# Moving the first layer's filter products and spectra into the start-up of a two-layer flow step

## The chip, the core and the metric

The kernel runs on one core of one Trainium2 chip. The metric is the time on the device in microseconds (us), here the median of three runs. TensorE (PE) multiplies matrices, VectorE (DVE), ScalarE (ACT) and GpSimd (POOL) work element by element, and SyncE (SP) issues the loads.

## The reference

Two trunk layers, each a mixer and a mixture of experts, over 128 context tokens and 256 latent tokens, 1024 features, float32. What the change touches is the filter of the Hyena group inside the mixer. It depends on the layer's parameters and on fixed tables alone, not on the tokens:

```python
def hyena_filter_spectrum(L, p):
    ...
    feats = jnp.concatenate([t[:, None], jnp.cos(ang), -jnp.sin(ang)], axis=-1)
    fr = p['hy_freq'].astype(f32)
    hid = jnp.sin(fr * (feats @ p['hy_w1'].astype(f32) + p['hy_b1'].astype(f32)))
    hid = jnp.sin(fr * (hid @ p['hy_w2'].astype(f32) + p['hy_b2'].astype(f32)))
    filt = (hid @ p['hy_w3'].astype(f32)).reshape(L, 2, HYENA_ORDER, D_HYENA)
    ...
    filt = filt * window[:, None, None, :]
    fwd, bwd = filt[:, 0], filt[:, 1]
    k = jnp.concatenate([fwd, jnp.zeros((1, HYENA_ORDER, D_HYENA), f32), bwd[:0:-1]], axis=0)
    return jnp.fft.rfft(k, axis=0)

def trunk_layer(x, cond, p, l, ctx_kv, ang):
    mod = cond @ p['w_mod'] + p['b_mod']
    sh1, sc1, g1, sh2, sc2, g2 = jnp.split(mod[:, None, :], N_MOD, axis=-1)
    h = rms_norm(x, p['g_pre_mix']) * (1.0 + sc1) + sh1
    y, k, v = mixer(h, p, l, ctx_kv, ang)
    ...
```

The spectrum is first used in `hyena_group`, after the projection `u = h @ p['w_in']`: the tokens' spectrum is multiplied by it, twice.

## The kernel before

The program is written out by hand: each engine has one list of instructions in a fixed order, and the engines wait for one another on counters (semaphores) by `wait_ge`. An engine that waits holds back everything behind it in its list. The loads of the start-up all go through SyncE's list, in the order written; `weight_in`, `mod_in` and the constants use one queue.

**Start-up of layer 0.** Twelve modulation chunks of 2 MB per layer (`mod_chunk`, L680) give the shifts, scales and gates; chunks 0 to 3 give the shift and scale of the mixer's norm. Their products gather in PSUM banks 6 and 7, are copied to SBUF (`mod_rows`), turned into columns by TensorE (`mod_columns`, L661), copied (`mod_column`) and applied while the transposed, normalised tokens (`to_features`, L824, banks 0 to 5) are copied out of PSUM by ScalarE and VectorE (`features`, L1320 and L1605). The small filter network is `hidden` (L691 and L694 on TensorE, L1867 to L1870 on VectorE, a sine on ScalarE).

**Projection stage.** 19 tiles (`u_tile`, `u_high` and `u_rest`, lines L896 to L924) in the loop over `i`, in the order `ORDER`, with PSUM banks 3 to 5. Tiles 2 to 9 are products of split weights: ScalarE copies the high part (`high`, L1449) into one of three buffers, and VectorE (tiles 2, 3) or GpSimd (tiles 4 to 9, L634) subtracts it. Between the tiles TensorE's list holds the filter work, for both layers alike: behind tiles 3, 4, 5 the filter blocks (`filters`, L703: two products of 128x512 into banks 1 and 2), which VectorE multiplies by the windows and adds and subtracts (L1879 to L1882, tiles FA and FB, which lie in QKV); behind tiles 6, 7, 8 the spectra (`spectra`, L717 and L721, banks 1 and 2), which ScalarE copies to KS (in KSYS, L1431). Behind tiles 9, 10 and 12 follow the turn, the spectrum and the inverse of the tokens (`z_turn`, `z_spectra`, `z_conv`), and again behind 13, 14 and 16. Each filter block waits for VectorE to have emptied the banks, each spectrum for ScalarE.

After that come attention, the output projection and the experts; layer 1 has the same stages, with `hidden` behind its first tiles.

Of the kernel before, what the change touches and what calls it, by code (L numbers as in the profile page):

```python
# [28 lines left out]
P = 128  # L29
# [34 lines left out]
_n = 0  # L64
for _name, _w in (("ident", 128), ("cond", 16), ("mean", 128), ("cf2", 512), ("sf2", 512), ("cf1", 128), ("sf1", 128),
                  ("ci2", 512), ("si2", 512), ("ci1", 128), ("si1", 128), ("win", 768), ("win0", 768),
                  ("cos", 64), ("sin", 64), ("tri", 64), ("iota", 384), ("before", 128), ("tokid", 3)):
    CONST[_name] = (_n, _n + _w)
    _n += _w
NCONST = _n  # L70
FIRST = CONST["cond"][1]
PAR = {}
# [29 lines left out]
def build(nc, I, O):  # L102
    lam_init = [0.8 - 0.6 * math.exp(-0.3 * l) for l in range(DEPTH)]
    with ExitStack() as ctx:
# [146 lines left out]
        NH3 = len(HALVED)  # L251
        FTB = ((0, 2, 4), (6, 0, 2))
        ROWB = (6, 6, 4, 6)
        COLB = (6, 5, 4, 5)
# [31 lines left out]
        def sem(name):  # L286
# [4 lines left out]

        const_in, x_in, par_in, ctx_in, kv_out, y_out = map(
            sem, ("const_in", "x_in", "par_in", "ctx_in", "kv_out", "y_out"))
        chunk_in = [sem(f"chunk_in{i}") for i in range(SLOTS + 1)]
# [116 lines left out]
        def _(sp):  # L411
# [37 lines left out]
            for l in range(DEPTH):  # L449
                if l == 0:  # L450
                    mod_in(0)
                    sp.dma_start(PR[:, :], I["par"][0]).then_inc(par_in, 16)
                    mod_in(1)
                    sp.dma_start(X[:, :, :], I["x"]).then_inc(x_in, 16)
                    mod_in(2)
                    mod_in(3)
                weight_in(l, "f1")
                if l == 0:
                    sp.dma_start(CST[:, FIRST:], I["consts"][:, FIRST:]).then_inc(const_in, 16)
                    sp.wait_ge(mod_used, 3)  # L460
# [191 lines left out]
        def _(pe):  # L652
# [43 lines left out]
            def filters(l, t):  # L696

                if t == 0:
                    pe.wait_ge(a_hid, 2 * l + 2)
                else:  # L700
                    pe.wait_ge(d_filt, K_FILT * l + 4 * t)
                for half in range(2):
                    mm = nc.tensor.matmul(PS[1 + half][:, :], HID[:, 4, t * P:(t + 1) * P],  # L703
                                          par("w3", 64)[:, half * 512:(half + 1) * 512], start=True, stop=True)
                mm.then_inc(pe_filt, 1)

            def spectra(l, q):

                if q == 0:
                    pe.wait_ge(const_in, 32)  # L710
                    pe.wait_ge(d_filt, K_FILT * l + K_FILT)
                else:
                    pe.wait_ge(a_spec, 6 * l + 2 * q)
                for part, f in ((0, FA), (1, FB)):
                    if q == 0:
                        w = cst("cf1" if part == 0 else "sf1")
                        mm = nc.tensor.matmul(PS[1 + part][:, :], w, f[:, 0, :], start=True, stop=True)  # L717
                    else:
                        w = cst("cf2" if part == 0 else "sf2").rearrange("p (t f) -> p t f", t=2)
                        for t in range(2):  # L720
                            mm = nc.tensor.matmul(PS[1 + part][:, :], w[:, t, (q - 1) * P:q * P], f[:, 1 + t, :],  # L721
                                                  start=(t == 0), stop=(t == 1))
                mm.then_inc(pe_spec, 1)

            def z_turn(l, o):

                if o == 0:
                    pe.wait_ge(a_spec, 6 * l + 6)
# [88 lines left out]
            def to_features(l, r, t):  # L817

                pe.wait_ge(d_xn, 6 * l + 3 * r + t + 1)
                if r == 1 and t > 0:  # L820
                    features_done(l, 1, t - 1)
                for half in range(2):
                    for k in range(4):
                        mm = nc.tensor.transpose(PS[FTB[r][t] + half][:, k * P:(k + 1) * P], XNK[r][:, t, 4 * half + k, :], ident)  # L824
                    mm.then_inc(pe_hT, 1)
# [324 lines left out]
            for l in range(DEPTH):  # L1150

                if l == 0:
                    pe.wait_ge(const_in, 16)
                    mod_chunk(0)
                    mod_chunk(1)
                    hidden(l, 0)
                    mod_chunk(2)
                    hidden(l, 1)
                    pe.wait_ge(d_arg, 8)
                    for t in range(NT):  # L1160
                        to_features(l, 0, t)
                    mod_chunk(3)
                    mod_columns(0)
                else:
                    for t in range(NT):
# [3 lines left out]
                for i in range(19):  # L1169
# [120 lines left out]
        def _(act):  # L1290
# [136 lines left out]
            def spectra(l, q):  # L1427

                act.wait_ge(pe_spec, NT * l + q + 1)
                for part in range(2):  # L1430
                    own.sig(sc.activation(KS[:, q, part, :, :].rearrange("p o n -> p (o n)"), PS[1 + part][:, :], ACT.Copy), a_spec)  # L1431

# [44 lines left out]
            for l in range(DEPTH):  # L1477
                act.wait_ge(par_in, 16 * (l + 1))
                if l == 0:
                    for t in range(NT):  # L1480
                        squares(l, 0, t)
                    hidden(l, 0)
                    hidden(l, 1)
                    mod_rows(0)
                    mod_column(0)
                    act.wait_ge(d_mod, 3)
                    for t in range(NT):
                        features(l, 0, t)
                else:
                    for t in range(NT):  # L1490
# [19 lines left out]
                for i in range(19):  # L1510
# [3 lines left out]
                    if 1 <= i < 7:  # L1514
                        high(l, i + 1)
                    if 6 <= i < 9:
                        spectra(l, i - 6)
# [72 lines left out]
        def _(dve):  # L1590
# [281 lines left out]
            def filters(l, t):  # L1872
# [3 lines left out]
                two = lambda ap: ap.rearrange("p (o n) -> p o n", o=2)  # L1876
                dve.wait_ge(const_in, 32)
                dve.wait_ge(pe_filt, NT * l + t + 1)
                sig(v.tensor_tensor(two(FW), two(PS[1][:, :]), win[:, t, :].unsqueeze(1).to_broadcast([P, 2, 256]), ALU.mult), d_filt)  # L1879
                do(v.tensor_tensor(two(BW), two(PS[2][:, :]), win0[:, t, :].unsqueeze(1).to_broadcast([P, 2, 256]), ALU.mult), d_filt)  # L1880
                sig(v.tensor_tensor(FA[:, t, :], FW, BW, ALU.add), d_filt)
# [102 lines left out]
            for l in range(DEPTH):  # L1984
# [274 lines left out]
```

## Time and profile before

| What | Value |
|---|---|
| runs | 1751.35, 1750.44, 1751.37 us; median 1751.35 |
| profiled execution, span | 1745.4 us from its first to its last instruction |
| profiled execution, own time | not recorded apart; the median lies 5.95 us above the span |
| TensorE busy | 1661.9 us, 95% |
| VectorE, ScalarE, GpSimd busy | 642.6 (37%), 387.3 (22%), 222.8 us (13%) |
| mean granted TensorE clock | 0.982 |
| TensorE's chain share | 89% |

The profile is of one execution. A row of a timeline gives the start in us from the span's start, the duration, the engine and line, what is written from what is read, how many instructions the row merges, and in brackets the engine's idle time before it and what ended that. One float32 matmul of the program stands in it as two records; L12 is line 12 of the kernel. Where a row's records overlap, the duration of the chain of waits is the one that adds up.

### The profile page before, as it was taken

To read this page: it belongs to the slowest core of one execution; us is meant where nothing else is said; L and a number is where in the kernel's file an instruction comes from. 1 tells how busy PE (TensorE), PEld (TensorE's weight loads), DVE (VectorE), ACT (ScalarE), POOL (GpSimd) and SP (SyncE) were. 2 spreads that over 40 slices of the span, in tenths; PEclk is the share of its full clock that TensorE was granted. 3 is DMA by queue.
4 is the path that set the end of the run, shared out by engine and by line. 5 is a ranking of instruction groups with operands and counts; after the bars stand their busy time and mean duration, and the time that the engine had idled before them with its cause. 6 is when DMAs were issued, how large, how long until landed. Compare 5 with 4: busy or idle time off the path is not lost.

```text
span 1745.4 us, 22336 instructions
## 1 busy us (share of the span) xinstructions
PE 1661.9 (95%) x8468; PEld 821.2 (47%) x8468; DVE 642.6 (37%) x1697; ACT 387.3 (22%) x842; POOL 222.8 (13%) x217
## 2 busy tenths in 40 slices
PE   4999889989999999999979998998999999999997
PEld 2765344644444444444447553555434444444443
DVE  2479372522222222222256765442322222222222
ACT  2410343221111111111152104431111111111111
POOL 0200010011111111111113000101111111111110
PEclk7999999999999999999989999999999999999999
DMA  9312753399999999999932229017899999999994
GB/s 403 133 54 102 279 210 145 126 403 374 417 403 413 417 388 419 420 420 419 381 128 97 103 97 375 23 60 310 338 418 416 396 420 396 412 419 420 419 420 166
DMA packets 77291, 530.52 MB, mean 304 GB/s; under 512 B 10880, under 2 KB 14080, under 8 KB 21632
## 3 DMA queue, kind: packets, MB, share of 16 engines
q1 hardware_dynamic: 67392, 503.90, 70.7%
q0 software_dynamic: 9792, 25.18, 3.7%
q8 instruction: 69, 1.13, 0.3%
q14 instruction: 38, 0.31, 0.1%
HBM read 533.76 MB, written 5.77 MB: 309 GB/s over the span
## 4 chain that ended last, share of the span: by engine, by line
PE 89%; DVE 4%; DMA 4%; ACT 2%; issue 1%; SPq 0%; POOL 0%; DVEq 0%; ACTq 0%
PE PSB L932 30%; PE PSB L941 15%; PE PSB L924 7%; PE PSB L986 6%; PE PSB L987 5%; PE PSB L974 4%; PE PSB L860 4%; DMA RING<-in_wmod 2%; PE PSB L896 1%; PE PSB L959 1%; PE PSB L919 1%; PE PSB L680 1%; PE PSB L906 1%; PE PSB L897 1%; DMA RING<-in_exp_w_up 1%; PE PSB L948 1%
## 5 line engine op out<-in xcount | busy, mean ns | idle before, releaser
L932 PE MATMUL PSB<-WB,EX 128*32 128x512 f32 (+2 forms) x1408 | 431.9, 598 | 0.6 <-DMA RING<-in_exp_w_up 0.6
L932 PE MATMUL PSB<-RING,EX 128*32 128x512 f32 (+2 forms) x1344 | 417.2, 598 | 1.7 <-DVE EX L1790 1.7
L941 PE MATMUL PSB<-RING,AT 128*32 128x512 f32 (+2 forms) x720 | 227.9, 599 | 4.8 <-ACT GROW L1299 3.7
L1808 DVE TENSOR_TENSOR YL<-PSB,YH 128x512 fp32r<-128x512 f32 x136 | 94.1, 692 | 353.8 <-ACT YH L1380 353.8
L941 PE MATMUL PSB<-WB,AT 128*32 128x512 f32 (+2 forms) x704 | 210.8, 596 | 0.0
L564 POOL TENSOR_SCALAR SCAT<-CST,LSTT 128x384 fp32r<-128x384 f32 x68 | 85.1, 1251 | 833.0 <-PE PSB L987 832.8
L932 PEld LDWEIGHTS PSB<-WB,EX 128*32 128x32 f32 (+2 forms) x1408 | 113.1, 126 | 136.3 <-issue 136.3
L986 PE MATMUL PSB<-YH,SCAT 128*128 128x512 f32 x408 | 171.6, 421 | 2.8 <-DVE YL L1808 2.8
L1790 DVE COPY EX<-PSB 128x512 f32<-128x512 f32 x68 | 47.1, 692 | 317.4 <-PE PSB L974 317.4
L932 PEld LDWEIGHTS PSB<-RING,EX 128*32 128x32 f32 (+2 forms) x1344 | 105.8, 124 | 122.5 <-issue 122.5
L987 PE MATMUL PSB<-YL,SCAT 128*128 128x512 f32 x408 | 161.0, 395 | 0.0
L1380 ACT ACTIVATE YH<-PSB 128x512 fp32r<-128x512 f32 x136 | 81.2, 597 | 239.5 <-PE PSB L941 239.5
L924 PE MATMUL PSB<-RING,HT 128*128 128x512 f32 x288 | 125.9, 592 | 0.0
L974 PEld LDWEIGHTS PSB<-CST,XG 128*128 128x128 f32 x544 | 58.9, 141 | 107.4 <-issue 105.4
L941 PEld LDWEIGHTS PSB<-RING,AT 128*32 128x32 f32 (+2 forms) x720 | 62.7, 129 | 78.4 <-issue 74.5
L1373 ACT ACTIVATE SGM<-PSB 128x256 f32<-128x256 f32 x68 | 26.1, 384 | 312.7 <-PE PSB L932 312.7
L941 PEld LDWEIGHTS PSB<-WB,AT 128*32 128x32 f32 (+2 forms) x704 | 58.4, 126 | 72.5 <-issue 72.0
L974 PE MATMUL PSB<-CST,XG 128*128 128x128 f32 x544 | 88.7, 286 | 1.4 <-ACT EX L1355 1.4
L556 POOL DMA_INDIRECT XG<-h_rows,IDX x68 | 74.7, 1098 | 113.3 <-DVE LSTW L1760 89.5
L986 PEld LDWEIGHTS PSB<-YH,SCAT 128*128 128x128 f32 x408 | 77.6, 190 | 21.1 <-issue 4.9
L860 PE MATMUL PSB<-RING,YT 128*128 128x512 f32 x192 | 86.5, 598 | 0.0
L924 PEld LDWEIGHTS PSB<-RING,HT 128*128 128x128 f32 x288 | 54.3, 190 | 63.0 <-issue 62.2
(286 smaller groups left out, 1856.6 us busy)
## 6 DMA issues: line engine op xcount, KB each, us to landing
RING<-in_exp_w_gate SPq DMA_DIRECT2D x64, 1024.0 KB, 12.4
RING<-in_exp_w_up SPq DMA_DIRECT2D x64, 1024.0 KB, 14.7
RING<-in_exp_w_down SPq DMA_DIRECT2D x64, 1024.0 KB, 13.1
WB<-in_exp_w_gate SPq DMA_DIRECT2D x64, 1024.0 KB, 11.7
WB<-in_exp_w_up SPq DMA_DIRECT2D x64, 1024.0 KB, 14.4
WB<-in_exp_w_down SPq DMA_DIRECT2D x64, 1024.0 KB, 13.3
RING<-in_wmod SPq DMA_DIRECT2D x16, 2048.0 KB, 10.6
KSYS<-in_wmod SPq DMA_DIRECT2D x8, 2048.0 KB, 10.4
```

The lines of the kernel that those rows point to most:

```text
L556: pool.indirect_dma_start(XG[:, s % 2, :], None, h_rows, bass.IndirectOffsetOnAxis(ap=IDX[:, s:s + 1], axis=0), bounds_check=TOK - 1, oob_ ...
L564: nc.gpsimd.tensor_scalar(SCAT[:, s % 2, :], cst("iota"), LSTT[:, s:s + 1], None, ALU.is_equal).then_inc(p_scat, 1)
L860: mm = nc.tensor.matmul(PS[YB[0][t] + hf][:, :], YT[:, f, t * P:(t + 1) * P], w[:, f, :], start=(f == 0), stop=(f == 7))
L924: mm = nc.tensor.matmul(PS[3 + i % 3][:, :], HT[:, k, t * P:(t + 1) * P], w[:, k, :], start=(k == 0), stop=(k == KD - 1))
L932: mm = nc.tensor.matmul(PS[6][s0:s0 + w, :].rearrange("p (w f) -> p w f", w=2), e[:, k, s0:s0 + w], rawgu[n % NBUF][:, k], start=(k == 0), ...
L941: mm = nc.tensor.matmul(dst[s0:s0 + w, :], AT[:, j, s0:s0 + w], rawdn[n % NBUF][:, hf, j], start=(j == 0), stop=(j == 1))
L974: mm = nc.tensor.transpose(PS[7][:, c * P:(c + 1) * P], XG[:, s % 2, k * P:(k + 1) * P], ident)
L986: nc.tensor.matmul(PS[piece][:, :], w, YHb[s % 2][:, cols], start=False, stop=False, skip_group_check=True)
L987: mm = nc.tensor.matmul(PS[piece][:, :], w, YLb[s % 2][:, cols], start=False, stop=True, skip_group_check=True)
L1380: sc.activation(YHb[s % 2][:, hf * 512:(hf + 1) * 512], PS[6 + hf][:, :], ACT.Copy).then_inc(a_yh, 1)
L1790: v.tensor_copy(EX2[:, s % 2, 4:8, :].rearrange("p k s -> p (k s)"), PS[7][:, :]).then_inc(e_high, 1)
L1808: v.tensor_tensor(YLb[s % 2][:, hf * 512:(hf + 1) * 512], PS[6 + hf][:, :], YHb[s % 2][:, hf * 512:(hf + 1) * 512].bitcast(F32), ALU.subtr ...
```

## The change

For layer 0 alone, the three filter blocks and the three spectra leave the loop over `i` and stand in the start-up, among the modulation chunks; both `hidden` steps stand ahead of chunk 0, and chunk 3 ahead of the transposes. Each filter block and each spectrum of layer 0 gets PSUM banks of its own (`FILTB`, `SPECB`), so most waits between them fall away; the transposes of tokens 0 and 1 wait for the copies of spectra 0 and 1, whose banks they take over. The constants are laid out anew in three parts with semaphores of their own (`win_in`, `dft_in`, `const_in`); the parameters and the windows load ahead of chunk 0, the Fourier tables behind chunk 1, the rest behind the first projection weights. VectorE does both `hidden` steps and the window products before it normalises the tokens; ScalarE does the sines before the squares, copies spectra 0 and 1 before `mod_rows`, and spectrum 2 behind `features`. Layer 1 is as before.

```diff
-for _name, _w in (("ident", 128), ("cond", 16), ("mean", 128), ("cf2", 512), ("sf2", 512), ("cf1", 128), ("sf1", 128),
-                  ("ci2", 512), ("si2", 512), ("ci1", 128), ("si1", 128), ("win", 768), ("win0", 768),
+for _name, _w in (("ident", 128), ("cond", 16), ("win", 768), ("win0", 768), ("cf2", 512), ("sf2", 512), ("cf1", 128),
+                  ("sf1", 128), ("mean", 128), ("ci2", 512), ("si2", 512), ("ci1", 128), ("si1", 128),
...
+        FILTB = ((0, 2, 4), (1, 1, 1))
+        SPECB = ((0, 2, 6), (1, 1, 1))
...
                 if l == 0:
+                    sp.dma_start(PR[:, :], I["par"][0]).then_inc(par_in, 16)
+                    sp.dma_start(CST[:, FIRST:WINDOWS], I["consts"][:, FIRST:WINDOWS]).then_inc(win_in, 16)
                     mod_in(0)
-                    sp.dma_start(PR[:, :], I["par"][0]).then_inc(par_in, 16)
                     mod_in(1)
+                    sp.dma_start(CST[:, WINDOWS:FORWARD], I["consts"][:, WINDOWS:FORWARD]).then_inc(dft_in, 16)
                     sp.dma_start(X[:, :, :], I["x"]).then_inc(x_in, 16)
...
                 if l == 0:
-                    sp.dma_start(CST[:, FIRST:], I["consts"][:, FIRST:]).then_inc(const_in, 16)
+                    sp.dma_start(CST[:, FORWARD:], I["consts"][:, FORWARD:]).then_inc(const_in, 16)
                     sp.wait_ge(mod_used, 3)
...
                 if t == 0:
                     pe.wait_ge(a_hid, 2 * l + 2)
-                else:
+                elif l > 0:
                     pe.wait_ge(d_filt, K_FILT * l + 4 * t)
                 for half in range(2):
-                    mm = nc.tensor.matmul(PS[1 + half][:, :], HID[:, 4, t * P:(t + 1) * P],
+                    mm = nc.tensor.matmul(PS[FILTB[l][t] + half][:, :], HID[:, 4, t * P:(t + 1) * P],
...
                 if q == 0:
-                    pe.wait_ge(const_in, 32)
+                    pe.wait_ge(dft_in, 16)
                     pe.wait_ge(d_filt, K_FILT * l + K_FILT)
-                else:
+                elif l > 0:
                     pe.wait_ge(a_spec, 6 * l + 2 * q)
+                elif q == 2:
+                    pe.wait_ge(a_col, 1)
...
                 pe.wait_ge(d_xn, 6 * l + 3 * r + t + 1)
+                if l + r == 0 and t < 2:
+                    pe.wait_ge(a_spec, 2 * t + 2)
...
                 if l == 0:
                     pe.wait_ge(const_in, 16)
+                    hidden(l, 0)
+                    hidden(l, 1)
                     mod_chunk(0)
+                    filters(l, 0)
                     mod_chunk(1)
-                    hidden(l, 0)
+                    filters(l, 1)
+                    filters(l, 2)
+                    spectra(l, 0)
                     mod_chunk(2)
-                    hidden(l, 1)
-                    pe.wait_ge(d_arg, 8)
+                    spectra(l, 1)
+                    mod_chunk(3)
                     for t in range(NT):
                         to_features(l, 0, t)
-                    mod_chunk(3)
                     mod_columns(0)
+                    spectra(l, 2)
...
-                    if 3 <= i < 6:
+                    if l > 0 and 3 <= i < 6:
                         filters(l, i - 3)
-                    if 6 <= i < 9:
+                    if l > 0 and 6 <= i < 9:
                         spectra(l, i - 6)
...
                 if l == 0:
+                    hidden(l, 0)
+                    hidden(l, 1)
                     for t in range(NT):
                         squares(l, 0, t)
-                    hidden(l, 0)
-                    hidden(l, 1)
+                    spectra(l, 0)
+                    spectra(l, 1)
                     mod_rows(0)
                     mod_column(0)
                     act.wait_ge(d_mod, 3)
                     for t in range(NT):
                         features(l, 0, t)
+                    spectra(l, 2)
...
                     scalars()
                     hidden(l, 0)
+                    hidden(l, 1)
+                    for t in range(NT):
+                        filters(l, t)
                     for t in range(NT):
                         normalise(l, 0, t)
-                    hidden(l, 1)
...
                 low(l, 1)
                 if l > 0:
                     hidden(l, 1)
-                for t in range(NT):
-                    filters(l, t)
+                    for t in range(NT):
+                        filters(l, t)
+                dve.wait_ge(const_in, 32)
                 short(l, 0)
```

TensorE's list before, from the program's start to the first projection tile (L919); L680 are modulation chunks of eight products, L691 and L694 the two `hidden` products, L824 the transposes, L661 `mod_columns`:

```order
L680 MATMUL PSB<-RING,COND 32x512 x16
L691 MATMUL PSB<-PR 64x384
L680 MATMUL PSB<-RING,COND 32x512 x8
L694 MATMUL PSB<-CO,PR 64x384
L824 MATMUL PSB<-CST,YT 128x128 x24
L680 MATMUL PSB<-RING,COND 32x512 x8
L661 MATMUL PSB<-FOLD,GROW 128x4 x8
L919 MATMUL PSB<-HT,RING 128x384 x16
```

The same stretch of TensorE's list now; L684 are the chunks, L707 the filter blocks (two products each), L723 and L727 the spectra, L833 the transposes, L665 `mod_columns`, L928 the first tile:

```order
L695 MATMUL PSB<-PR 64x384
L698 MATMUL PSB<-CO,PR 64x384
L684 MATMUL PSB<-RING,COND 32x512 x8
L707 MATMUL PSB<-PR,CO 128x512 x2
L684 MATMUL PSB<-RING,COND 32x512 x8
L707 MATMUL PSB<-PR,CO 128x512 x4
L723 MATMUL PSB<-QKV,CST 128x512 x2
L684 MATMUL PSB<-RING,COND 32x512 x8
L727 MATMUL PSB<-QKV,CST 128x512 x4
L684 MATMUL PSB<-RING,COND 32x512 x8
L833 MATMUL PSB<-CST,YT 128x128 x24
L665 MATMUL PSB<-FOLD,GROW 128x4 x8
```

Behind these twelve rows stand spectrum 2 (L727, four products) and the first tile; filter blocks 1 and 2 stand together, and spectrum 0 ahead of chunk 2.

SyncE's list of loads before, from the start to the last first-stage weights; columns are float32, 128 rows each:

```order
L448 DMA CST<-in_consts 128x144
L417 DMA RING<-in_wmod 128x4096
L452 DMA PR<-in_par 128x2100
L417 DMA RING<-in_wmod 128x4096
L454 DMA X<-in_x 128x3072
L417 DMA RING<-in_wmod 128x4096 x2
L429 DMA RING<-in_wfm 128x4096
L459 DMA CST<-in_consts 128x4931
L429 DMA RING<-in_wfm 128x2048
L429 DMA RING<-in_wfm 128x4096
```

The same stretch of SyncE's list now:

```order
L450 DMA CST<-in_consts 128x144
L453 DMA PR<-in_par 128x2100
L454 DMA CST<-in_consts 128x1536
L419 DMA RING<-in_wmod 128x4096 x2
L457 DMA CST<-in_consts 128x1280
L458 DMA X<-in_x 128x3072
L419 DMA RING<-in_wmod 128x4096 x2
L431 DMA RING<-in_wfm 128x4096
L463 DMA CST<-in_consts 128x2115
L431 DMA RING<-in_wfm 128x2048
L431 DMA RING<-in_wfm 128x4096
```

The parameters (2100 columns) and the windows (1536) have moved ahead of all modulation chunks, the Fourier tables (1280) ahead of X; the loads are the same bytes in all.

## Rows read from the trace of the kernel before

**Rows 1.** TensorE timeline: start us, us, line, out<-in, count, idle before it
```profile
8.95 3.28 PE L680 MATMUL PSB<-RING,COND 128*32 128x512 f32 x16 [8.95 <-DMA RING<-in_wmod]
16.30 3.64 PE L680 MATMUL PSB<-RING,COND 128*32 128x512 f32 x16 [4.07 <-DMA RING<-in_wmod]
19.87 1.54 PE L691 MATMUL PSB<-PR 17*64 17x384 f32 x2
24.89 3.64 PE L680 MATMUL PSB<-RING,COND 128*32 128x512 f32 x16 [3.48 <-DMA RING<-in_wmod]
...
31.59 4.56 PE L824 MATMUL PSB<-CST,YT 128*128 128x128 f32 x24 [2.12 <-DVE CO L1870]
36.08 1.92 PE L680 MATMUL PSB<-RING,COND 128*32 128x512 f32 x16
38.72 1.95 PE L661 MATMUL PSB<-FOLD,GROW 128*128 128x4 f32 x16 [0.72 <-ACT GROW L1411]
46.01 1.65 PE L919 MATMUL PSB<-HT,RING 128*128 128x384 f32 x2 [5.34 <-ACT HT L1320]
```

**Rows 2.** DMA issues before 130 us: count, KB each, us to landing
```profile
RING<-in_wmod SPq DMA_DIRECT2D x4, 2048.0 KB, 11.9
...
CST<-in_consts SPq DMA_DIRECT2D x1, 2465.5 KB, 20.8
X<-in_x SPq DMA_DIRECT2D x1, 1536.0 KB, 17.4
PR<-in_par SPq DMA_DIRECT2D x1, 1050.0 KB, 9.7
```

**Rows 3.** Stretches: us, TensorE busy (records), granted clock, DMA share, GB/s
```profile
28.00:29.00 1.00, 1.00 (x6) 0.60 1.04 442
...
35.00:36.00 1.00, 1.00 (x8) 0.68 0.97 414
...
42.00:43.00 1.00, 0.00 (x0) 0.73 0.96 410
...
217.00:218.00 1.00, 0.49 (x4) 1.00 0.88 377
218.00:219.00 1.00, 0.08 (x1) 1.00 1.15 492
```

**Rows 4.** Chain of waits in two stages: start us, us, what
```profile
66.53 1.92 PE PSB L703 x4
...
85.44 1.72 PE PSB L717 x4
...
91.39 3.43 PE PSB L721 x8
...
106.59 0.65 PE PSB L734 x6
...
196.67 11.68 DMA RING<-in_wmod
```

**Rows 5.** TensorE's timeline once the first projection tiles are under way
```profile
49.65 8.55 PE L919 MATMUL PSB<-HT,RING 128*128 128x384 f32 x26
```

**Rows 6.** VectorE's timeline, window multiplications of the third filter block
```profile
81.21 0.69 DVE L1879 TENSOR_TENSOR QKV<-PSB,CST 128x512 f32<-128x512 f32 x1 [3.16 <-PE PSB L703]
81.82 0.68 DVE L1880 TENSOR_TENSOR QKV<-PSB,CST 128x512 f32<-128x512 f32 x1
82.53 1.18 DVE L1881 TENSOR_TENSOR QKV<-QKV 128x512 f32<-128x512 f32 x1
83.64 0.68 DVE L1882 TENSOR_TENSOR QKV<-QKV 128x512 f32<-128x512 f32 x1
```

**Rows 7.** GpSimd's timeline at the same place: a weight split
```profile
80.77 2.40 POOL L634 TENSOR_TENSOR RINGL<-RING,GROWH 128x1024 fp32r<-128x1024 f32 x1 [3.87 <-ACT GROWH L1449]
```

**Rows 8.** ScalarE's timeline: a weight split's copy, and a spectrum's two copies
```profile
79.63 1.06 ACT L1449 ACTIVATE GROWH<-RING 128x1024 fp32r<-128x1024 f32 x1
...
87.19 1.09 ACT L1431 ACTIVATE KSYS<-PSB 128x512 f32<-128x512 f32 x2 [0.60 <-PE PSB L717]
```

More of the change, by code:

```diff
@@ L70 @@
 NCONST = _n
-FIRST = CONST["cond"][1]
+FIRST, WINDOWS, FORWARD = CONST["cond"][1], CONST["win0"][1], CONST["sf1"][1]
 PAR = {}
@@ L289, in sem @@
             return sems[name]
-        const_in, x_in, par_in, ctx_in, kv_out, y_out = map(
-            sem, ("const_in", "x_in", "par_in", "ctx_in", "kv_out", "y_out"))
+        const_in, win_in, dft_in, x_in, par_in, ctx_in, kv_out, y_out = map(
+            sem, ("const_in", "win_in", "dft_in", "x_in", "par_in", "ctx_in", "kv_out", "y_out"))
         chunk_in = [sem(f"chunk_in{i}") for i in range(SLOTS + 1)]
@@ L716, in spectra @@
                         w = cst("cf1" if part == 0 else "sf1")
-                        mm = nc.tensor.matmul(PS[1 + part][:, :], w, f[:, 0, :], start=True, stop=True)
+                        mm = nc.tensor.matmul(PS[SPECB[l][q] + part][:, :], w, f[:, 0, :], start=True, stop=True)
                     else:
@@ L720, in spectra @@
                         for t in range(2):
-                            mm = nc.tensor.matmul(PS[1 + part][:, :], w[:, t, (q - 1) * P:q * P], f[:, 1 + t, :],
+                            mm = nc.tensor.matmul(PS[SPECB[l][q] + part][:, :], w[:, t, (q - 1) * P:q * P], f[:, 1 + t, :],
                                                   start=(t == 0), stop=(t == 1))
@@ L727, in z_turn @@
                 if o == 0:
+                    pe.wait_ge(const_in, 32)
                     pe.wait_ge(a_spec, 6 * l + 6)
@@ L1430, in spectra @@
                 for part in range(2):
-                    own.sig(sc.activation(KS[:, q, part, :, :].rearrange("p o n -> p (o n)"), PS[1 + part][:, :], ACT.Copy), a_spec)
+                    own.sig(sc.activation(KS[:, q, part, :, :].rearrange("p o n -> p (o n)"), PS[SPECB[l][q] + part][:, :], ACT.Copy), a_spec)
             def z_out(l, o):
@@ L1515, in _ @@
                         high(l, i + 1)
-                    if 6 <= i < 9:
+                    if l > 0 and 6 <= i < 9:
                         spectra(l, i - 6)
@@ L1876, in filters @@
                 two = lambda ap: ap.rearrange("p (o n) -> p o n", o=2)
-                dve.wait_ge(const_in, 32)
+                dve.wait_ge(win_in, 16)
                 dve.wait_ge(pe_filt, NT * l + t + 1)
-                sig(v.tensor_tensor(two(FW), two(PS[1][:, :]), win[:, t, :].unsqueeze(1).to_broadcast([P, 2, 256]), ALU.mult), d_filt)
-                do(v.tensor_tensor(two(BW), two(PS[2][:, :]), win0[:, t, :].unsqueeze(1).to_broadcast([P, 2, 256]), ALU.mult), d_filt)
+                sig(v.tensor_tensor(two(FW), two(PS[FILTB[l][t]][:, :]), win[:, t, :].unsqueeze(1).to_broadcast([P, 2, 256]), ALU.mult), d_filt)
+                do(v.tensor_tensor(two(BW), two(PS[FILTB[l][t] + 1][:, :]), win0[:, t, :].unsqueeze(1).to_broadcast([P, 2, 256]), ALU.mult), d_filt)
                 sig(v.tensor_tensor(FA[:, t, :], FW, BW, ALU.add), d_filt)
```

## The prediction

> **What bounds the kernel now.** I read first the busy line of the page: TensorE is busy 95% of the span, so the time moves only where TensorE waits or where work leaves it. Then its timeline from the start to the first projection tile [rows 1]: the reader is to see four modulation chunks (L680), and gaps of 8.95, 4.07, 3.48, 2.12, 0.72 and 5.34 us. The first three end with a weight chunk landing; the 2.12 us end with VectorE's work on the filter network, the 5.34 us with the normalised features. The first projection tile starts at 46.01 us; I call that moment S. Behind S the chain of waits runs on TensorE alone up to the attention, and in it stand the filter products and spectra that the change moves [rows 4]. So the question is what they cost behind S, what they cost ahead of it, and what the loads now bring later.
>
> **What leaves the stage behind S.** Three filter blocks of 1.92 us (one row stands for the three), the first spectrum 1.72 us, the second and third 3.43 us each (one row for the two) [rows 4]: 5.76 + 1.72 + 6.86 = 14.3 us, all at the full clock and all on the chain. What could take their place is a projection tile that waits for its split weights. A split is a ScalarE copy of 1.06 us and a GpSimd subtraction of 2.40 us [rows 7, 8], 3.5 us behind the release of a buffer three tiles back; two tiles lie between, and each spends about 4.2 us (from 85.44 + 1.72 to 91.39, one tile [rows 4]). So I cost the shorter stage at nothing: the cover of 8.4 us is over twice the split. Everything behind the tenth tile (short convolutions, the 62 taps, attention, experts) is started by TensorE's progress, so it moves as one block. The attention's wait of 11.68 us for a modulation chunk [rows 4] is such a case: its load is issued when a chunk ahead of it is used, hence it moves too and gives nothing back.
>
> **When the loads land now.** They pass one queue in order. From the chunk that landed at 16.30 to the one at 24.89 us [rows 1] the queue moved X and a chunk, 1536 + 2048 KB [rows 2]: 2.40 us per 1000 KB. Counting back, the landing time is 16.3 + 0.0024 x (KB so far - 5218). The new order is 72, parameters 1050, windows 768, chunk 0, chunk 1, Fourier tables 640, X, chunk 2, chunk 3, first weights (2048 each chunk). So: parameters 6.5 us, windows 8.3, chunk 0 13.2 (was 8.95), chunk 1 18.1 (16.30), tables 19.7, X 23.4, chunk 2 28.3 (24.89), chunk 3 33.2, first projection weights 38.1, rest of the constants 40.6, second weights 43.1 as before. The weights are there well ahead of S, and the constants ahead of the short convolutions that now wait for them. The queue stays fed: chunk 3 is issued when chunk 1 has been used, near 22 us, with chunk 2 in flight until 28.3.
>
> **TensorE ahead of S, step by step.** A modulation chunk takes 3.64 us at 1.2 GHz and 1.92 at 2.4; the first hidden product 1.54 [rows 1] and the second no more. With the parameters at 6.5 us both hidden products, with VectorE's and ScalarE's part between, are through by about 14.5.
> - 13.2: chunk 0, low clock, 3.6. 16.9: filter block 0. Its clock is not shown by the trace. In the trace the clock rose about 4 us into unbroken work: at 28.8 for work from 24.89 and at 35.6 for work from 31.59 [rows 1, 3], yet it had not risen within the 5.1 us from 16.30. I take half of the block at each level, 2.9 us, to 19.8.
> - Chunk 1 1.9, filter blocks 1 and 2 3.8: to 25.5. Each block has its own two PSUM banks, so none waits for VectorE.
> - VectorE multiplies: a block's four operations start 0.61 and 0.71 us apart, the third took 1.18 us beside GpSimd's split and the fourth 0.68 [rows 6]. Without GpSimd I take 0.61 + 0.71 + 0.65 + 0.68 = 2.65 us a block. Block 1 is ready for it at 23.6, so block 2 is through at 28.9. The first spectrum waits for that: a new gap of 3.5 us on TensorE, with chunk 1 used up, chunk 2 landed at 28.3 and queued behind the spectrum.
> - Spectrum 0, after that gap at the low clock: 3.4, to 32.4. Chunk 2, part low part full: 2.8, to 35.2. Spectrum 1 3.4, to 38.6; its ScalarE copies (1.09 us [rows 8]) end ahead of the transposes that now wait for their banks. Chunk 3 1.9, to 40.5.
> - The 24 transposes took 4.56 us, mostly at the low clock; six like them take 0.65 at the full one [rows 1, 4]: 2.6, to 43.1. Mod columns 1.95 to 45.1. From their end to S it was 5.34 us, ScalarE and VectorE work that is unchanged: S = 50.4, later by 4.4 us.
> - Spectrum 2 (3.4 us) lies inside these 5.34 us: free.
>
> In the gap ahead of S the clock fell (at 42.5 [rows 3]), and the first six records of the first tile took 3.64 us where the next 26 took 8.55, 0.33 each [rows 1, 5]: 1.7 us lost. Now spectrum 2 fills that gap and leaves 1.9 us idle; between 217 and 219 us TensorE was idle for 0.51 + 0.92 us and the clock stayed full [rows 3]. I take the 1.7 us as saved.
>
> Sum: -14.3 + 4.4 - 1.7 = -11.6 us, 0.7%. The profiled span is 1745.4; its own full time is not recorded, the median of the runs lies 5.95 us above the span, and I leave that distance alone. So 1739.8 us.
>
> **Where a rule speaks against it.** The trace shows the clock down after each long gap and up again some 4 us into work [rows 1, 3]. The Trainium skill (TensorE: Matmul & The Clock Gate, "What's actually happening") says that half rate is the default and that only sustained activity lifts it. The trace agrees on the direction. By that rule alone, with every piece up to chunk 2 at half rate because gaps still stand before and among them, the sum would be that of rival 2; by the rises in the rows it is the one above.
>
> **The sum's bounds.** Best: full clock from filter block 1 to S (spectrum 0 1.7 and chunk 2 1.9 instead of 6.2 us) and half of filter block 0's doubt: S at 46.9 to 47.8: -14.2 to -15.1 us, down to 1736.2. Worst of the same course: no clock saving at S, chunk 2 wholly low (+0.8), filter block 0 wholly low (+0.9), VectorE's third operations held up in two blocks by GpSimd's small powers, as much as beside the split (1.18 against 0.68 [rows 6], +1.0): -7.2 us, 1744.1.
>
> **Rivals.**
> 1. *The clock stays full through the gap* (the idle 3.5 us cost nothing): 1737.2. The sum is then -14.3 - 1.7 + 1.8 (S at 47.8), and up to 0.9 better with the doubts of the bounds. For it: the idle piece near 218 us was harmless [rows 3]. Against: it fell in the gap of 5.34 us. Chance 0.15.
> 2. *Half the saving is eaten by the low clock.* If chunk 1 and all filter blocks run low, they end at 32.0, VectorE at 34.7, spectrum 0 at 38.1, chunk 2 at 41.8; then full: spectrum 1 45.2, chunk 3 47.1, transposes 49.7, columns 51.7, S 57.0. -14.3 + 11.0 - 1.7 = -5.0: 1746.3. For it: the 5.1 us from 16.30 that stayed low. Chance 0.08.
> 3. *Slower.* One mechanism: the clock is low from chunk 0 to the last transpose, in a start-up that now holds 14 us more of TensorE's work. Then as in rival 2 up to 41.8, and spectrum 1 6.9, chunk 3 3.6, transposes 5.3, columns 1.95, gap 5.34: S = 64.9, later by 18.9, and no clock saving: +4.6, 1756.0. It decides from the point at which S is later by over 14.3. Against it: the old start-up, with less work and more gaps, rose twice. Chance 0.03.
> 4. *The shortened stage waits.* The work leaves the stage behind S and a wait for split weights takes its place; then only the later S is left, up to 1751.35 + 4.4 = 1755.8, or no change if half of it stays. Against it is the cover of 8.4 us over 3.5; for it only that GpSimd once shares with VectorE. Chance 0.04.
>
> **How the numbers follow.** The forecast has 0.70, rivals 1 to 4 have 0.15, 0.08, 0.03 and 0.04. A difference of 0.2%, 3.5 us, is about what a measurement tells from none. Faster: 0.70 + 0.15 + 0.08 = 0.93; rival 4 splits evenly: same 0.02, slower 0.02 + 0.03 = 0.05. The range 1735.5 to 1745.0 holds the forecast's bounds and rival 1, and leaves out rivals 2 to 4.
>
> **What would show it.** In the new profile: chunk 0 starting near 13.2 us and chunk 1 no earlier than 18.1; a TensorE gap near 25.5 that ends with VectorE's FB; spectrum 2 between mod columns and the first tile; S near 50; the tenth tile's end near 46 us behind S where it was 60.6 us (106.59 - 46.01). The prediction is wrong if S is beyond 55, if tiles 4 to 9 wait for RINGL, or if the block behind the tenth tile is not the old one shifted.

## The result, and the profile of the changed kernel

The changed kernel took 1735.15 us (median of four runs, 1729.62 to 1735.58) against 1750.89 us for the kernel before (four runs, 1749.41 to 1751.37): ratio 0.9906, 95% interval 0.989 to 0.9921. Measured again later, with six runs against seventeen, it was 1735.34 against 1748.61: 0.9930, interval 0.9917 to 0.9943, which is 10.0 to 14.5 us faster. One of the six took 3455.48 us, twice the others, and nothing on record says why; the readings below leave it out. The forecast was 1739.8, range 1735.5 to 1745.0. The direction held and, as the traces show, most of the steps; the number lies 0.35 us below the range.

TensorE's timeline of the changed kernel up to the first projection tile (L928), columns as in [rows 1]. L695 and L698 are the hidden products, L684 the chunks, L707 the filter blocks, L723 and L727 the spectra, L833 the transposes, L665 the columns:

```profile
6.30 1.50 PE L695 MATMUL PSB<-PR 17*64 17x384 f32 x2 [6.30 <-DMA PR<-in_par]
11.89 1.54 PE L698 MATMUL PSB<-CO,PR 64*64 64x384 f32 x2 [4.08 <-ACT CO L1439]
13.36 3.48 PE L684 MATMUL PSB<-RING,COND 128*32 128x512 f32 x16
16.77 1.99 PE L707 MATMUL PSB<-PR,CO 64*128 64x512 f32 x4
18.68 1.92 PE L684 MATMUL PSB<-RING,COND 128*32 128x512 f32 x16
20.54 3.70 PE L707 MATMUL PSB<-PR,CO 64*128 64x512 f32 x8
28.07 3.75 PE L723 MATMUL PSB<-QKV,CST 128*128 128x512 f32 x4 [3.83 <-DVE QKV L1899]
31.75 2.82 PE L684 MATMUL PSB<-RING,COND 128*32 128x512 f32 x16
34.50 3.70 PE L727 MATMUL PSB<-QKV,CST 128*128 128x512 f32 x8
38.13 1.92 PE L684 MATMUL PSB<-RING,COND 128*32 128x512 f32 x16
39.98 2.96 PE L833 MATMUL PSB<-CST,YT 128*128 128x128 f32 x24
42.78 1.85 PE L665 MATMUL PSB<-FOLD,GROW 128*128 128x4 f32 x16
44.91 3.70 PE L727 MATMUL PSB<-QKV,CST 128*128 128x512 f32 x8 [0.29 <-ACT MODC L1433]
```

The three gaps that ended with a chunk's landing in [rows 1] are gone. Ahead of chunk 0 TensorE now waits for the parameters and for the small filter network (6.30 and 4.08 us); behind it one long gap is left, 3.83 us, which ends with VectorE's last sum of filter block 2 (L1899). Behind it spectrum 0 (four records) takes 3.75 us, which is the price at 1.2 GHz ([rows 4] has 1.72 at full clock), and chunk 2 is half and half. The granted clock shows it, columns as in [rows 3]:

```profile
26.00:27.00 1.00, 0.00 (x0) 0.89 0.96 410
27.00:28.00 1.00, 0.00 (x0) 0.50 1.05 442
...
33.00:34.00 1.00, 1.00 (x12) 0.69 1.04 442
```

VectorE's part, as in [rows 6]: with GpSimd idle or nearly so the third operation (L1898) takes 0.69 us where it took 1.18, and a block 2.61 us (25.30 to 27.91; 2.65 forecast).

```profile
25.30 0.69 DVE L1896 TENSOR_TENSOR QKV<-PSB,CST 128x512 f32<-128x512 f32 x1
...
25.91 0.68 DVE L1897 TENSOR_TENSOR QKV<-PSB,CST 128x512 f32<-128x512 f32 x1
...
26.62 0.69 DVE L1898 TENSOR_TENSOR QKV<-QKV 128x512 f32<-128x512 f32 x1
...
27.23 0.68 DVE L1899 TENSOR_TENSOR QKV<-QKV 128x512 f32<-128x512 f32 x1
```

The chain of waits through the projection stage (start us, us, what); L928 stands for the first 32 records of the stage, L915 for the last part of a tile, L741 for the turn; the rows left out are the single products L905 and L906 between them, one behind the other:

```profile
49.88 10.59 PE PSB L928 x32
...
66.02 2.78 PE PSB L915 x16
...
71.63 1.41 PE PSB L915 x8
...
75.81 1.39 PE PSB L915 x8
...
79.97 1.39 PE PSB L915 x8
...
84.19 1.42 PE PSB L915 x8
...
88.38 1.39 PE PSB L915 x8
...
92.54 1.39 PE PSB L915 x8
93.93 0.66 PE PSB L741 x6
```

Tiles 4 to 9 follow one another every 4.2 us with nothing between them. The stage's first 32 records take 10.59 us where they took 12.19 [rows 1, 5]. The list of TensorE's waits in this stage has one entry, the 1.3 us ahead of tile 0; none for split weights.

What each trace says about where time was saved, in us from its span's start (S is the first tile, "turn" what follows the tenth; "experts" the first scatter product of layer 0; the last column is the last scatter product of layer 1; the own time is that of the profiled execution, which need not be near the kernel's median):

| Kernel | own time | span | S | turn | experts | last scatter |
|---|---|---|---|---|---|---|
| before, the profile above | not given | 1745.4 | 46.0 | 106.4 | 384.4 | 1733.5 |
| before_again | 1750.7 | 1748.9 | 46.3 | 106.9 | 384.7 | 1736.9 |
| changed | 1734.8 | 1733.0 | 49.9 | 93.8 | 371.8 | 1721.1 |
| after_again | 1735.1 | 1733.3 | 49.5 | 93.3 | 371.5 | 1721.4 |
| changed_look | 1733.5 | 1731.7 | 53.4 | 97.2 | 371.9 | 1719.7 |
| loads_only | 1746.5 | 1744.7 | 49.2 | 109.5 | 385.0 | 1732.7 |
| filters_only | 1738.3 | 1736.5 | 46.9 | 101.2 | 376.7 | 1724.6 |
| spectrum2_back | 1741.4 | 1739.6 | 53.5 | 102.3 | 377.7 | 1727.7 |
| gap_filled | 1732.6 | 1730.7 | 47.6 | 91.5 | 369.0 | 1718.8 |
| gap_look | 1730.0 | 1728.1 | 48.4 | 92.3 | 368.5 | 1716.2 |
| gap_filled_warm | 1731.7 | 1729.7 | 46.8 | 90.7 | 368.4 | 1717.8 |
| x_behind_chunk2 | 1736.5 | 1734.7 | 49.5 | 93.4 | 370.7 | 1722.8 |
| x_behind_warm | 1729.6 | 1727.8 | 46.5 | 90.3 | 366.7 | 1715.9 |
| x_behind_filled | 1733.4 | 1731.5 | 46.9 | 90.8 | 369.9 | 1719.7 |

Between the two profiles the change is 12.7 us at the turn, 12.6 at the experts, 12.4 at the end. So the traces say 12.4 and the first medians 15.7, and that is what had to be explained.

### The profile page after: what moved, and what is told of

The parts are those of the page before. It is cut to its first block, busy times and chain, and to the rows that moved or that the text cites. A ratio compares the mean times of both kernels' runs of the same rounds, so it can differ in the third digit from the quotient of the medians.

```text
span 1733.0 us, 22340 instructions
## 1 busy us (share of the span) xinstructions
PE 1657.6 (96%) x8468; PEld 818.9 (47%) x8468; DVE 649.9 (38%) x1697; ACT 386.5 (22%) x842; POOL 221.6 (13%) x217
## 4 chain that ended last, share of the span: by engine, by line
PE 91%; DVE 4%; ACT 2%; DMA 2%; issue 1%; POOL 0%; DVEq 0%; SPq 0%; ACTq 0%
PE PSB L941 31%; PE PSB L950 15%; PE PSB L933 7%; PE PSB L995 6%; PE PSB L996 5%; PE PSB L983 4%; PE PSB L869 4%; PE PSB L684 2%; PE PSB L968 1%; PE PSB L905 1%; PE PSB L928 1%; PE PSB L915 1%; PE PSB L906 1%; PE PSB L957 1%; PE PSB L819 1%
## 5 line engine op out<-in xcount | busy, mean ns | idle before, releaser
L933 PEld LDWEIGHTS PSB<-RING,HT 128*128 128x128 f32 x288 | 54.3, 190 | 63.0 <-issue 62.2
## 6 DMA issues: line engine op xcount, KB each, us to landing
RING<-in_exp_w_gate SPq DMA_DIRECT2D x64, 1024.0 KB, 12.4
```

The costliest lines, as they stand in the source:

```text
L933: mm = nc.tensor.matmul(PS[3 + i % 3][:, :], HT[:, k, t * P:(t + 1) * P], w[:, k, :], start=(k == 0), stop=(k == KD - 1))
```

## The experiments

**The kernel before against itself.** No edit.

> The kernel before, run again against itself. The two profiles differ by 12.4 us of span (1745.4 and 1733.0), the medians by 15.7 us. Theory A: the profiled execution of before was a quick one; its runs have spans near 1749, some 4 us above 1745.4, and about 1.8 us lie outside the span in every run. Theory B: the spans of before are all near 1745.4 and 5.5 us lie outside it, against 1.8 us in the changed kernel: the change shortens what lies outside the span. The ratio is 1.000 by both.

Its twelve runs went from 1743.1 to 1750.7, median 1748.3; the span of every run lies 1.8 to 2.0 us below its time (1750.7 and 1748.9; 1747.2 and 1745.4), as in the changed kernel (1734.8 and 1733.0). So theory B falls, and of theory A the 1.8 us outside the span hold: with them the first profile, span 1745.4, was an execution of 1747.2 us, 4.15 us quicker than the median it was held against. The other half of theory A doesn't hold. The spans are not near 1749: their median is 1746.4, only 1 us above the profiled one. The larger part of the 4.15 us is that the three first runs were slow for this kernel. The later medians of the kernel before are 1748.61, 1748.77, 1749.28 and 1749.15 us, 48 runs in all, and four of these 48 reach 1751.35. Where do two executions of one kernel part? At the experts of layer 0 they are 0.3 us apart, at the end 3.4; they part in layer 1's attention. TensorE's timeline there, in the first profile of before:

```profile
1065.26 2.52 PE L680 MATMUL PSB<-RING,COND 128*32 128x512 f32 x16 [2.63 <-DMA RING<-in_wmod]
...
1070.34 1.92 PE L680 MATMUL PSB<-KSYS,COND 128*32 128x512 f32 x16
```

and in the second, before_again:

```profile
1065.17 1.92 PE L680 MATMUL PSB<-RING,COND 128*32 128x512 f32 x16 [2.05 <-DMA RING<-in_wmod]
...
1071.37 3.64 PE L680 MATMUL PSB<-KSYS,COND 128*32 128x512 f32 x16 [2.64 <-DMA KSYS<-in_wmod]
```

The same chunk costs 1.92 or 3.64 us, as the clock falls or not around the gap ahead of it. A quick chunk can also meet its successor's load too early and wait.

**The changed kernel again, twice.** No edit.

> The changed kernel again. Both theories: 0.991, median near 1735. It is the mark for the other two kernels of this call, and shows how often the quick run of 1729.6 us comes.

> The changed kernel, for a third trace. By the forecast's steps: first tile between 49.3 and 50.0, its tenth tile's end near 93.8, and the rest of the distance to another run made in the two attention stages.

after_again: 1735.34 us, near 1735 as expected; but for the one of 3455 us its runs lie between 1735.0 and 1737.7, and a quick one like the 1729.6 us of the first call is not among them. The ratio is 0.993, not the 0.991 expected, since the kernel before took 1748.61 us in this call and not 1750.89. changed_look missed on the start-up: the first tile at 53.4 and the turn at 97.2, 3.4 us later than forecast for it. Its timeline of TensorE's start-up shows why:

```profile
13.43 3.64 PE L684 MATMUL PSB<-RING,COND 128*32 128x512 f32 x16
17.00 3.78 PE L707 MATMUL PSB<-PR,CO 64*128 64x512 f32 x4
20.70 3.64 PE L684 MATMUL PSB<-RING,COND 128*32 128x512 f32 x16
24.28 4.27 PE L707 MATMUL PSB<-PR,CO 64*128 64x512 f32 x8
```

Filter block 0 and chunk 1 ran at the low clock, at twice their price: the mechanism of rival 2, seen. Filter blocks 1 and 2 took 4.27 us together where the full clock takes 3.70, so the clock rose early in them, and the first tile is at 53.4 and not at rival 2's 57.0. It is a matter of the execution, not of the kernel. Its whole run was none the longer (1733.5): the stages between turn and experts took 274.7 us where the first profile of the changed kernel has 278.0. The two traces show where. Up to 128.7 us behind the turn they keep the same distance, so the loads that the attention waits for gave nothing back. Then the first profile spends 5.34 us from its `mod_columns` (L665) at 222.84 us to the next L1235 product, at the low clock from 225 to 228 us, and changed_look 3.78. The rest, 1.7 us, lies in the first weight products of the experts, in the first profile

```profile
298.93 5.38 PE L941 MATMUL PSB<-RING,HT 128*128 128x512 f32 x8
```

and in changed_look

```profile
300.72 3.68 PE L941 MATMUL PSB<-RING,HT 128*128 128x512 f32 x8
```

In the first profile the granted clock fell there although TensorE was never idle (columns as in [rows 3]):

```profile
300.00:301.00 1.00, 1.00 (x3) 0.50 0.04 16
```

So the late first tile was made good by the clock, which fell twice in one execution where it stayed up in the other. No trace ties this to the start-up: it is luck.

**Only the loads.** Everything but the order of loads, the layout and the semaphores goes back:

```diff
-                    hidden(l, 0)
-                    hidden(l, 1)
                     mod_chunk(0)
-                    filters(l, 0)
                     mod_chunk(1)
-                    filters(l, 1)
-                    filters(l, 2)
-                    spectra(l, 0)
+                    hidden(l, 0)
                     mod_chunk(2)
...
-                    if l > 0 and 3 <= i < 6:
+                    if 3 <= i < 6:
```

> Only the new order of the loads and the new layout of the constants; the products, copies and waits are in the order of the kernel before. Theory A (all of the later start comes from 1408 KB ahead of chunk 2): chunk 2 lands at 28.3 instead of 24.9 us and the first tile starts at 49.4 instead of 46.0: 3.4 us slower than before, 0.2%. Rival: the loads come in time even so, since the gaps ahead of the chunks are not what sets the end: no change.

Ratio 1.0014, interval 1.0003 to 1.0024: slower by some 2.5 us where 3.4 were expected. In its trace chunk 2 starts with its landing, 28.28 us (forecast 28.3), and the first tile at 49.22, later by 3.2. The rival falls by the trace, and by an interval that ends just above 1. The trace is of a quick run (1746.5 us, median 1751.35), so its last columns in the table say nothing of the cost.

```profile
28.28 3.63 PE L684 MATMUL PSB<-RING,COND 128*32 128x512 f32 x16 [5.79 <-DMA RING<-in_wmod]
...
49.22 11.11 PE L924 MATMUL PSB<-HT,RING 128*128 128x384 f32 x29 [5.33 <-ACT HT L1325]
```

**Only the filter blocks moved.**

```diff
                     filters(l, 2)
-                    spectra(l, 0)
                     mod_chunk(2)
-                    spectra(l, 1)
                     mod_chunk(3)
...
                     mod_columns(0)
-                    spectra(l, 2)
...
-                    if l > 0 and 6 <= i < 9:
+                    if 6 <= i < 9:
```

ScalarE's copies move with the products, here and in the next experiment.

> The changed kernel, but the three spectra of layer 0 stay between the projection tiles 6, 7 and 8; the filter blocks alone are in the start-up. Theory A: the start-up is then bound by chunks 2 and 3 (28.3 and 33.2 us): first tile at 45.6 and, with an empty gap ahead of it, at the low clock (1.7 us); the spectra's 8.6 us are back behind it. Against before: -5.8 for the filter blocks and -0.4 for the start, 6.2 us faster, ratio 0.9965. Rival (the start-up waits for VectorE's window products also without the spectra): first tile past 47, under 5 us faster.

Ratio 0.9957, interval 0.9942 to 0.9973: 7.5 us faster, 6.2 expected and inside the interval. Its stage from first tile to turn is 54.3 us long against 60.4 before and 43.9 in the changed kernel: 6.1 us for the filter blocks (5.8 priced), 10.4 for the spectra and the clock of the first tile (8.6 + 1.7 priced). The first tile came at 46.9, not 45.6: chunk 3 ran low behind its gap, which costs 1.7 us. Chunk 2 ran low too, but chunk 3 still had to wait 1.25 us for its load:

```profile
28.54 3.64 PE L684 MATMUL PSB<-RING,COND 128*32 128x512 f32 x16 [4.04 <-DMA RING<-in_wmod]
33.44 3.64 PE L684 MATMUL PSB<-RING,COND 128*32 128x512 f32 x16 [1.25 <-DMA RING<-in_wmod]
```

Set beside loads_only, this run shows a third part of the change, which the prediction did not price by itself. Both have the same loads, yet here the first tile is 2.3 us earlier, with the filter blocks ahead of it. The hidden products stand ahead of chunk 0 and chunk 3 ahead of the transposes, and the 2.12 us for which the transposes waited for VectorE's part of the filter network ([rows 1], and 2.12 us again in loads_only) are gone.

**Spectrum 2 back behind tile 8.**

```diff
                     mod_columns(0)
-                    spectra(l, 2)
...
-                    if l > 0 and 6 <= i < 9:
+                    if 6 <= i < 9 and (l > 0 or i == 8):
```

> The changed kernel, but the third spectrum of layer 0 (TensorE's products and ScalarE's copies) stands behind tile 8 again. Theory A (the gap ahead of the first projection tile gives both the free 3.4 us and the clock): the spectrum costs 3.4 us on the path, and with the gap of 5.3 us empty again the clock falls, so that the first tile loses 1.7 us: 5.1 us slower than the changed kernel, 1740. Rival: the clock saving was not real or comes from elsewhere: 3.4 us slower, and the first six records of the first tile stay near 0.33 us each.

1740.04 us, 4.7 slower than the changed kernel in the same call (5.1 expected, rival 3.4). The gap ahead of the first tile is whole again and the tile pays for it, 12.07 us for its 32 records against 10.59 by the chain:

```profile
53.47 12.07 PE L926 MATMUL PSB<-HT,RING 128*128 128x384 f32 x32 [5.26 <-ACT HT L1331]
```

That row overlaps the next by a little; the stage as a whole is 48.8 us against 43.9, and 4.9 is 3.4 for the spectrum and 1.5 for the clock. Both terms stand by the trace; the medians alone could hardly tell 4.7 from the rival's 3.4. This trace too has the start-up at the low clock through chunk 1, as changed_look has: its first tile is 3.6 us later than in the first profile of the changed kernel, and that is no part of what the spectrum costs.

**The gap filled with idle products.** Behind `filters(l, 2)`:

```diff
+                    pe.wait_ge(d_filt, 4)
+                    for _ in range(15):
+                        nc.tensor.matmul(PS[0][:, 0:P], ident, ident, start=True, stop=True)
```

> The changed kernel, with 15 products of the identity by itself put into TensorE's gap between filter block 2 and spectrum 0 (24.2 to 28.0 us); their result is used by nothing. Theory A (the low clock behind that gap costs 1.8 us on spectrum 0 and 0.9 on chunk 2): both run at the full clock, 2.7 us faster than the changed kernel, near 1732.6. Rival (the clock is not the gap's doing, or the time is bound by chunk 3's landing at 33.2): no change, or slower by what the products overrun the gap.

> The kernel gap_filled again, for a second trace. Its runs spread from 1731.7 to 1742.6 us where the changed kernel's lie within 1735 to 1738. Theory A (whether the clock is up by filter block 0 differs between executions, as it did in the profiled run of x_behind_chunk2): a run under 1734 has filter block 0 in 2.0 us and the first tile near 47.6; a run over 1737 has filter blocks of 3.8 us, or chunk 1 at 3.6, and the first tile at 50 or later. Rival (the spread is made in the attention): the first tile near 47.6 in either.

The traced run did as theory A says: spectrum 0 and chunk 2 at the full clock, first tile at 47.60, 1732.6 us.

```profile
24.59 3.62 PE L1172 MATMUL PSB<-CST 128*128 128x128 f32 x30
28.48 1.96 PE L723 MATMUL PSB<-QKV,CST 128*128 128x512 f32 x4 [0.28 <-DVE QKV L1902]
30.37 1.93 PE L684 MATMUL PSB<-RING,COND 128*32 128x512 f32 x16
```

But its six runs spread from 1731.7 to 1742.6, median 1735.64: no gain over the changed kernel by that. The second look caught a run of 1729.96 us, not one near 1740, so no slow run of this kernel was seen. It missed theory A even so, which wanted the first tile of such a run near 47.6 and filter block 0 at 2.0 us. It has 48.4 and 2.65, and was yet 2.6 us quicker than the first look: the block from turn to last scatter took 3.4 us less. That part of the spread is made behind the start-up, as the rival says.

**The same, with the clock raised early.** Nine more idle products between the two hidden products:

```diff
                     hidden(l, 0)
+                    for _ in range(9):
+                        nc.tensor.matmul(PS[5][:, 0:P], ident, ident, start=True, stop=True)
                     hidden(l, 1)
```

> gap_filled with 9 more idle products between the two hidden products. Theory A: the clock is up in every execution by filter block 0, so the slow half of gap_filled's runs (1737.7 to 1742.6) goes: median 1732.5, all within 1735. Rival (attention): the spread of 11 us and the median of 1735.6 stay.

Median 1732.21, all runs within 1731.7 to 1732.8; ratio 0.9907, interval 0.9891 to 0.9924. The spread of 11 us shrank to 1.1, and chunk 0 already runs at the full clock:

```profile
8.18 4.21 PE L1165 MATMUL PSB<-CST 128*128 128x128 f32 x18
12.33 1.09 PE L698 MATMUL PSB<-CO,PR 64*64 64x384 f32 x2
13.52 1.92 PE L684 MATMUL PSB<-RING,COND 128*32 128x512 f32 x16
```

That fits theory A; with four runs, no trace of a run near 1740, and several us of spread seen behind the start-up elsewhere, I call it supported, not shown.

**X behind chunk 2.**

```diff
-                    sp.dma_start(X[:, :, :], I["x"]).then_inc(x_in, 16)
                     mod_in(2)
+                    sp.dma_start(X[:, :, :], I["x"]).then_inc(x_in, 16)
...
-                    spectra(l, 0)
                     mod_chunk(2)
+                    spectra(l, 0)
```

> The changed kernel, but X is loaded behind modulation chunk 2, and TensorE takes chunk 2 ahead of the first spectrum, where it now waits for VectorE. Chunk 2 then lands at 24.6 instead of 28.3 us. Theory A (the start-up is bound by TensorE's own list with its gap of 3.8 us and the low clock that follows it): the gap is filled, a gap of 1.5 us is left, spectrum 0 and chunk 2 run at the full clock: the first tile starts near 45.5 instead of 49.9, 4.4 us faster than the changed kernel, near 1731. Rival C (the normalised tokens, which need X, become the bound: X at 28.3, squares to 33, transposes from 35): no gain or under 1 us.

> The kernel with X behind chunk 2, and 9 idle products of the identity between the two hidden products, before chunk 0. In the profiled run of x_behind_chunk2 (1736.5 us, its other runs 1728.5 to 1731.5) the clock stayed low up to 28.3 us. Theory A (whether the clock is up at chunk 0 differs from execution to execution): with more work ahead it is up in all of them: all runs within 1728 to 1732, median 1729.5. Rival: the slow run had another cause: the spread of 8 us stays.

> x_behind_warm with 7 idle products also between chunk 2 and spectrum 0, where its trace has a gap of 1.98 us. Theory A: chunk 1 and spectrum 2, which ran at the low clock in that trace, run at the full one in more executions: first tile at 45 to 46, median 1729, all runs within 3 us. Rival (the attention stages alone make the spread by now): median 1730 and a spread near 5 us, as for x_behind_warm.

x_behind_chunk2 took 1730.57 us, ratio 0.9896 (0.9882 to 0.991), 4.8 us below the changed kernel of the same call: theory A's 4.4, and not rival C's gain of under 1 us. Its profile happened to be of its slowest run (1736.5; the others 1728.5 to 1731.5), with a low clock up to the last two filter blocks:

```profile
16.95 3.78 PE L707 MATMUL PSB<-PR,CO 64*128 64x512 f32 x4
20.66 3.64 PE L684 MATMUL PSB<-RING,COND 128*32 128x512 f32 x16
24.23 4.34 PE L707 MATMUL PSB<-PR,CO 64*128 64x512 f32 x8
28.50 1.93 PE L684 MATMUL PSB<-RING,COND 128*32 128x512 f32 x16
```

Those two took 4.34 us where the full clock takes 3.70, so the clock rose some 1.3 us into them, near 25.5 us, and not at 28.3 as the expectations read it. The first tile of this run is at 49.5, as in the changed kernel; a quick run of this kernel was not traced, and the 45.5 us of theory A were not seen. The nearest is x_behind_warm, with a gap of 1.98 us ahead of spectrum 0 and the first tile at 46.5.

With the nine idle products (x_behind_warm) the median is 1730.03, 1727.7 to 1732.6, ratio 0.9893 (0.9877 to 0.991): no run reaches 1736.5 any more, though chunk 1 still ran low in its trace (3.45 us), and the median is no clear gain over the plain form's 1730.57. Seven more behind chunk 2 (x_behind_filled) gave 1730.85, 1729.8 to 1733.4, ratio 0.9889: nothing more, the rival's outcome; now chunk 2 ran low (3.51 us) behind a gap of 0.91. All three beat both kernels, by about 5 us against the changed one; their intervals lie apart from its later one.

## Why the prediction was wrong in its number, and which steps held

- **The step that failed** is the carrying over: "the median of the runs lies 5.95 us above the span, and I leave that distance alone". The distance was 5.95 us for the three runs of the kernel before and 2.15 for the changed kernel (median 1735.15, span 1733.0). That is 3.8 of the miss of 4.65 us; the other 0.8 is the sum, -11.6 forecast and -12.4 between the two profiles. Only 1.8 us of the distance lie outside the span. The other 4.15 were two draws: the profiled execution was 1.4 us quicker than the median of the seventeen later runs (1748.61), and the three runs had a median 2.7 us above it. The same sum, added to 1745.4 + 1.8, gives 1735.6, where the profiled execution of the changed kernel took 1734.8; and 11.6 us lie inside the later interval of 10.0 to 14.5. The range had no term for this: it held only what the change might do, not what the anchor might be.
- **What leaves the stage**: -16.0 forecast with the first tile's clock, -16.5 in the traces (60.4 to 43.9). filters_only and spectrum2_back show the parts. The half microsecond over is not placed; filters_only puts 0.3 of it with the filter blocks.
- **The later start**: +4.4 forecast, +3.9 found. The landings were within 0.3 us (chunk 2 28.28 in loads_only for 28.3, chunk 3 33.44 in filters_only for 33.2). Filter block 0 ran at the full clock in this trace (1.99 us, I had halved it at 2.9), spectrum 0 at the low one (3.75 for 3.4), chunk 2 half (2.82 for 2.8), the gap on VectorE was 3.83 us for 3.5. That it came out so near is in part luck: in changed_look, the same kernel, the first tile is 7.4 us later than before.
- **A size that was too small in the worst bound**: VectorE's third operation beside GpSimd was put at 1.18 us. In the same trace the one of filter block 0 took 2.15, because GpSimd worked on two splits in a row (rows in the last section). In the changed kernel it never came to that, 0.69 each.
- **Rivals.** 1: its full clock through the gap did not come in any of the three traces of the changed kernel; gap_filled shows what it would be worth, 2.3 us at the first tile. 2: its low clock through chunk 1 came in changed_look and in spectrum2_back, but ended early in filter blocks 1 and 2, and in changed_look two stretches at the full clock later in the run, by luck, made up for it. 3: refuted by every trace; even changed_look has the full clock from 36 to 49 us. 4: refuted, no tile waited for split weights.
- **The block behind the tenth tile moves as one**: true to 0.3 us from turn to end in the two profiles of the forecast, but not in general. From turn to last scatter the two traces of the kernel before took 1627.1 and 1630.0 us, the three of the changed kernel 1627.3, 1628.1 and 1622.5.

## What to carry to other kernels

Find out which run the profile is of before its span is used as an anchor: put what lies outside the span on the span, and hold a forecast against that sum, or widen the range by the spread of the kernel's own runs. Take more than three runs for the anchor where the forecast is under 1%. Work moved into a stage that waits for loads can be cheap: here 14.3 us of work started the first tile 3.9 us later, and the new order of the loads alone cost 3.2. But its price has to be written at both clock levels, and the engine behind it (here VectorE) may open a new gap that lowers the clock for what follows. Among loads that pass one queue, the one needed first by the longest chain goes first: a swap of two loads and two products gave, in the medians, as much again as a third of the whole change.

## What the runs showed of the hardware

- One kernel's executions have TensorE's clock up at different places. The first filter block of the changed kernel, at the same moment of the start-up, took 1.99 us in one execution and 3.78 in another; a modulation chunk in layer 1's attention took 1.92 or 3.64.
- The clock also fell in unbroken work. In the first profile of the changed kernel the granted clock was 0.50 from 300 to 303 us with TensorE busy all the time; in the 3 us before, it had run products of 64 and 4 columns (L857, L665). Eight records of 512 columns then took 5.38 us, in changed_look 3.68.
- The granted clock doesn't tell them apart at the start: it reads 1.00 from 13 to 26 us in the profiles of changed_look and x_behind_chunk2, while their chunks take 3.64 us. There the durations are to be believed.
- VectorE's third window operation, whose two inputs both lie in SBUF, did not end before GpSimd's subtraction had: in the kernel before it took 2.15, 1.20 and 1.18 us and ended 0.5 us behind the subtraction each time. The two operations ahead of it read PSUM and took 0.69 and 0.68 us beside the same subtraction [rows 6, 7]. In the changed kernel's start-up all take 0.69 or 0.68. The first of the three, VectorE and GpSimd (two splits in one row):

```profile
69.88 2.15 DVE L1881 TENSOR_TENSOR QKV<-QKV 128x512 f32<-128x512 f32 x1
...
66.76 4.72 POOL L634 TENSOR_TENSOR RINGL<-RING,GROWH 128x1024 fp32r<-128x1024 f32 x2 [4.53 <-ACT GROWH L1449]
```

- The distance between a run's time and its span was 1.8 to 2.0 us in every run of every kernel.
